# Dense tile pairs of the differential attention spread over the whole mixed attention stream

## What is computed

```
# sparse branch, 8 heads of width 64: compressed keys (32 blocks), all earlier keys, and a window of 512
p_c = masked_softmax(q @ kc.T - slope * dist)          # 32 compressed blocks
p_s = masked_softmax(q @ ks.T - slope * dist)          # all 1024 keys (16 blocks are chosen of 16)
p_w = masked_softmax(q @ kw.T - slope * dist)          # 512 keys back
o_a = g0 * p_c @ vc + g1 * p_s @ vs + g2 * p_w @ vw
# differential branch, 4 heads of width 2 x 64, values of width 128
a   = p[0] - lam * p[1]                                # two causal softmaxes of one head
o_b = rms(a @ vd) * subln * (1 - lam_init)
```

## Time and profile before

| | |
|---|---|
| time before, median of 3 runs | 2198.32 us (2197.31 to 2204.06) |
| the profiled execution: time, span | 2206.14 us, 2204.3 us |
| PE busy over the span | 2027.6 us (92%) |
| DVE, ACT, POOL busy over the span | 1129.4 us (51%), 617.4 us (28%), 114.6 us (5%) |
| mean granted TensorE clock | 0.957 |
| attention stream | from 710 to 1152 us of the span |

### The profile page before, as it was taken

The page is one execution under the profiler, slowest core; times in us unless marked ns, Lnnn a source line. Parts: engine busy times, 40 slices in busy tenths (PEclk is TensorE's granted clock), DMA queues, the critical chain, the costliest instruction groups (busy, mean ns, idle before and its releaser), DMA issues. The chain is left out here.

```text
span 2204.3 us, 33715 instructions
## 1 busy us (share of the span) xinstructions
PE 2027.6 (92%) x12602; PEld 1822.9 (83%) x12602; DVE 1129.4 (51%) x2509; ACT 617.4 (28%) x1220; POOL 114.6 (5%) x176
## 2 busy tenths in 40 slices
PE   6989999998995899999898969699999999999997
PEld 1338888878995788888898957499999999999996
DVE  0434333332235677776766634455555555555555
ACT  2123333421223566775551022211111101111012
POOL 1021000001300000000300000000000000000000
PEclk9989999998996899999999989899999999999998
DMA  9755555321101000000003440311110111101104
GB/s 320 263 187 173 161 150 158 102 80 49 49 1 62 1 1 1 1 1 1 1 15 113 141 144 39 96 58 29 57 57 29 57 38 48 57 29 57 38 1 154
DMA packets 132538, 166.44 MB, mean 76 GB/s; under 512 B 15851, under 2 KB 98635, under 8 KB 132372
## 3 DMA queue, kind: packets, MB, share of 16 engines
q1 hardware_dynamic: 117790, 134.75, 19.2%
q0 software_dynamic: 4832, 17.15, 2.5%
q10 hardware_dynamic: 9808, 13.11, 1.8%
HBM read 144.31 MB, written 22.77 MB: 76 GB/s over the span
## 5 line engine op out<-in xcount | busy, mean ns | idle before, releaser
L1622 DVE TENSOR_TENSOR late_x<-late_x,ffn_po 128x344 f32<-128x344 f32 x528 | 244.3, 509 | 116.0 <-PE ffn_po L1552 115.7
L787 PE MATMUL nsa_out<-zs_z,nsa_probT 128*128 128x64 f32 (+1 forms) x1344 | 179.3, 280 | 5.2 <-DVE zs_z L944 4.9
L1535 PE MATMUL ffn_pg<-late_words_hi,ffn_uhi 128*128 128x344 f32 x528 | 169.3, 321 | 14.6 <-DVE ffn_ulo L1586 14.6
L1496 ACT ACTIVATE ffn_sg<-ffn_pg 128x344 f32<-128x344 f32 x66 | 30.2, 458 | 533.6 <-PE ffn_pg L1535 533.6
L787 PEld LDWEIGHTS nsa_out<-zs_z,nsa_probT 128*128 128x128 f32 x1344 | 172.3, 201 | 8.0 <-DVE zs_z L944 7.8
L1552 PE MATMUL ffn_po<-ffn_a_hi,ffn_ohi 128*128 128x344 f32 x528 | 169.0, 320 | 0.2 <-DVE late_x L1622 0.2
L1535 PE MATMUL ffn_pg<-late_words_lo,ffn_uhi 128*128 128x344 f32 x528 | 169.1, 320 | 0.0
L1535 PE MATMUL ffn_pg<-late_words_hi,ffn_ulo 128*128 128x344 f32 x528 | 169.1, 320 | 0.0
L1552 PE MATMUL ffn_po<-ffn_a_hi,ffn_olo 128*128 128x344 f32 x528 | 168.9, 320 | 0.0
L1535 PE MATMUL ffn_pv<-late_words_hi,ffn_uhi 128*128 128x344 f32 x528 | 168.8, 320 | 0.0
L1535 PE MATMUL ffn_pv<-late_words_lo,ffn_uhi 128*128 128x344 f32 x528 | 168.7, 319 | 0.0
(11 more groups left out here) (452 smaller groups left out, 4520.9 us busy)
## 6 DMA issues: line engine op xcount, KB each, us to landing
mod_wr<-in_w_ada SPq DMA_DIRECT2D x12, 2048.0 KB, 8.9
ffn_raw_u<-in_w_ffn_in SPq DMA_DIRECT2D x44, 512.0 KB, 5.6
kin_kin<-in_cache_kv SPq DMA_DIRECT2D x64, 256.0 KB, 3.5
ffn_raw_o<-in_w_ffn_out SPq DMA_DIRECT2D x22, 512.0 KB, 3.6
gate_d<-dec_gate ACTq DMA_DIRECT2D x48, 172.0 KB, 2.6
late_x<-gate_d SPq DMA_DIRECT2D x8, 1032.0 KB, 5.4
dec_raw<-in_w_in POOLq DMA_DIRECT2D x16, 512.0 KB, 5.5
dec_vin<-in_cache_kv SPq DMA_DIRECT2D x64, 128.0 KB, 2.2
```

Of the source, the lines that this page charges most:

```text
L787: mm = pe.matmul(out[jb.group % 2][:, jb.b, 0:w], probT[t % 2][:, q, :], g.z[:, jb.k0 // P + q, at:at + w], start=(q == 0), stop=(q == til ...
L1496: act.activation(sg[(j + c) % 2][:], pg[(j + c) % 2][:, 0:TCH], ACT.Silu).then_inc(silu_done, 1)
L1535: mm = pe.matmul(bank[b][:, 0:TCH], w[j][:, v * KD + k, :], h[:, k, tok], start=(k == 0 and q == 0), stop=(k == KD - 1 and q == 2))
L1622: dve.tensor_tensor(total[:, k, tok], total[:, k, tok], po[u % 4][:, 0:TCH], ALU.add).then_inc(o_read, 1)
```

## The change

The test for the next dense tile no longer counts all tiles (`group`) but a new counter `done`, which only sparse tiles raise.

```diff
-    p = group = 0
+    p = group = done = 0
...
             group += 1
+            done += 1
             if x == 1:
                 items.append(("two queries", 0))
                 items.append(("two queries", 1))
-            if p < len(pairs) and not due and group * len(pairs) > p * LEAD:
+            if p < len(pairs) and not due and done * len(pairs) > p * LEAD:
                 j, i = pairs[p]
```

## The result

The changed kernel takes 2218.68 us (median of 5 runs, 2216.77 to 2220.23) against 2204.06 us of the kernel before (median of 5 beside it). The ratio is 1.0068 with an interval of 1.0053 to 1.0084: slower by 0.7%, where 0.5% faster was forecast and 2201 us was the upper end of the range. The five include the three of the table ahead of the prediction, whose median of 2198.32 us lies low: in the three later sessions the kernel before had medians of 2205.39, 2205.90 and 2206.01 us. The profiled execution took 2216.77 us with a span of 2215.0 us, 10.7 us longer than that of the kernel before.

A forecast was written before the change was run, and what follows sets the result against it. PE was taken to bound the kernel, with only its idle time and clock to win. Terms 8.8 + 1.7 - 1.5 - 1.0 + 3.0 = 11.0 us gained, from 2198.3 to 2187.3 us; range 2177 to 2201.

The forecast's parts named there:

- What bounds the kernel: Attention stream: PE bounds it, parts with and without dense tiles loaded almost alike; only 42.9 us idle and clock can be won.
- The waits by dense tiles: Five kinds of PE wait in the part with dense tiles, 17.5 us together; half, 8.8 us, forecast gained.
- The crowding: DVE bursts and closely set tiles at head starts; three reasons why spreading dense tiles shortens PE's waits, 8.8 us gained.
- (1): Start of heads 1 to 3: DVE's query remainders, compressed step and a large dense tile no longer stand in one row.
- (2): Sparse and dense tiles in turn: a sparse tile's values get one job more of slack before the finish they wait for.
- (3): Copies after the largest dense tiles: mostly followed by tiles 3, 4 and 5 instead of small tiles 0 and 1.
- the second queries: Second queries' preparation, once directly behind the first queries with no unit between to cover remainders: 1.0 us lost, bounds 0 and 3.6.
- POOL's normalisation: Start of head 6: table scalings find POOL idle, 3.7 us gained; less 2.0 for joins beside POOL, net 1.7 us.
- The cost of joins beside POOL: Joins of D7 and D0 beside POOL's normalisation: 2.0 us lost, bounds 0 and 4.7 us.
- The square root: First root, now straight before the copies of Q6: table load 1.28 and root 0.22 us, whole 1.5 us charged.
- The clock: TensorE at reduced clock in four short stretches of the stream: fewer falls from fewer waits, 3.0 us gained, bounds 8.4 either way.
- B: Rival: slower, 2209 us, by root, normalisation and joins crossing at Q6 in head 5, with two more clock falls; chance 0.10.

The follow-up runs named there:

- LAG 4 kernel: Changed order with every job turned four jobs after its scores instead of three, five probability buffers instead of four; 2192.12 us, ratio 0.9944 to the kernel before.
- the even order: The changed kernel's order of dense and sparse tiles, against the kernel before: 2218.68 us, ratio 1.0068, with every job turned three jobs after its scores.
- LAG 3: Every job turned three jobs after its scores, as in the kernel before (2204.06 us) and the changed kernel (2218.68 us).
- kernel before with join first: Kernel before with the join of a dense tile placed ahead of the maximum of the same job instead of behind it: 2205.95 us, ratio 1.0010.
- LAG 4 in the order before: Kernel before with every job turned four jobs after its scores instead of three, five probability buffers instead of four: 2224.87 us, ratio 1.0096.

## Why the prediction was wrong

**What bounds the kernel: right.** PE bounds the stream, the work of the two parts is alike, and only idle time and clock can change. The account above is this step in numbers: a rest of 361 to 370 us in every kernel of the table.

**The waits by dense tiles: the step that failed.** I set their bounds at 0 and 17.5 us of gain, with "each dense tile brings its waits with it" as the worst. A kind of wait can also grow, and the join's did, by 13.7 us. The sum had 8.8 us gained here, and the sign to watch was that the waits on the copies, the finish, the join and the maxima add up to about 9 us; from 745 us on they were 18.3 and are 28.8. The rows for it were there: the earlier trace rows has the join with the longest wait of these kinds, 1.5 us, and that wait was the one place in the kernel before where the next job but two was not a dense tile (D3 at the end of sparse head 3, s0a behind it):

```profile
997.92 0.31 PE L752 MATMUL nsa_sc<-at_kk,nsa_qhi 128*128 128x128 f32 x1
998.07 0.27 PE L752 MATMUL nsa_sc<-at_kk,nsa_qlo 128*128 128x128 f32 x1
...
999.03 0.75 DVE L986 SCALAR_TENSOR_TENSOR nsa_prob<-nsa_prob,nsa_factor 128x512 f32<-128x512 f32 x1
...
999.84 1.12 PE L769 MATMUL nsa_tp<-g_ident,nsa_prob 128*128 128x128 f32 x4 [1.50 <-DVE nsa_prob L986]
```

I read it as a leftover of crowding. It was the price of a join with little cover, and the change made 26 places with a sparse unit third, 13 of which wait. I had counted how far the finish and the values stand apart, in jobs, and not what PE has to do in the third job.

**The crowding: right, and small.** What reasons (1) and (2) would do is there, though no run takes them apart: finish and maxima fell by 3.9 us. The copies (3) did not fall (6.9 to 7.6 us), and the second queries cost 2.5 us (0.6 to 3.1), where I had 1.0.

**POOL's normalisation: right.** The scalings take 0.28, 0.69 and 0.49 us in all heads now and the 3.7 us are gone, as this view by line shows beside the earlier trace rows:

```profile
L938 DVE TENSOR_TENSOR nsa_share<-nsa_share,a_G x64: 160/161/1680, 749.0 to 1164.1; 128x2 f32<-128x2 f32 x64
...
L1028 DVE TENSOR_SCALAR at_tcmp<-at_tcmp x8: 283/285/288, 717.5 to 1119.7; 128x256 f32<-128x256 f32 x8
L1028 DVE TENSOR_SCALAR at_tsel<-at_tsel x8: 684/688/689, 717.7 to 1119.9; 128x1024 f32<-128x1024 f32 x8
L1028 DVE TENSOR_SCALAR at_twin<-at_twin x8: 486/488/490, 718.3 to 1120.5; 128x640 f32<-128x640 f32 x8
```

The cost of joins beside POOL was almost nil here, by luck: D7 was joined ahead of the normalisation, and D0 in 0.40 us, since the POOL instruction beside it ended 0.25 us after the join began. L938 right behind it took 1.68 us. In the LAG 4 kernel the two did meet, and D0's join took 1.40 us instead of 0.35:

```profile
1035.95 2.37 POOL L734 TENSOR_TENSOR zs_z<-zs_z,c_subln 128x1024 f32<-128x1024 f32 x1
1037.07 1.40 DVE L987 SCALAR_TENSOR_TENSOR nsa_prob<-nsa_prob,nsa_factor 128x128 f32<-128x128 f32 x1
```

The Trainium skill ("GPSIMD Engine Reference", section "8. Key points") says that VectorE instructions with two SBUF inputs contend with GpSimd; the join has two, and this row agrees. It did not decide this change.

**The square root: too dear.** PE waited 1.11 us for the queries at Q6 in head 5, against 1.05 before, and I had put 2.5. The waits for the queries' remainder grew by 2.4 us in all, but mostly in heads 1, 2 and 4.

**The clock: wrong sign.** I expected fewer and shorter waits, so 3.0 us back. The waits became longer (three of at least 1.2 us before, nineteen after, in the list of single waits), and 4.2 us more of the clock went missing: eight falls behind the start-up instead of four. Four of the eight begin within about 2 us of a join wait of 1.4 to 1.7 us (those ending at 901.7, 917.9, 1016.8 and 1035.3 us).

**The rivals.** B was the only one on the right side, but by a crossing at Q6; the run with root and QQ2 moved away was 1.2 us faster, which is within what sessions differ by. The profiled executions differ by 10.7 us of span, with 9.1 of waits and 4.2 of clock less 2.9 of the rest; the medians differ by 14.6, and no trace shows the other 3.9 us.

**The starting time.** I took 2198.3 us, the median of three, while the profiled execution had 2206.1. From the 2204 to 2206 us of later sessions the same sum gives 2193 to 2195, and the measured time stays as far off.

## What to carry to other kernels

When an order of jobs changes under a fixed distance between stages, look at each hand-over and write down what the waiting engine has to do in the jobs between, in microseconds; at a distance of three jobs the third job's scores alone were 2.1 us at one place and 0.4 at another, and all of PE's work after the second job's scores 3.1 or 1.5 us for the same pair of dense tiles. A wait that stands once in the old trace, at the one place that looks like the new order, says the sign of what the new order costs, and only coarsely its size: 1.5 us at 26 places would be 39 us, and 17.3 us in 15 places came of it. Order and distance are to be tried together: the even order lost 0.7% with LAG 3 and won 0.6% with LAG 4, while the old order lost 1.0% with LAG 4.

## What was not expected of the hardware

No single wait of the changed kernel in this stream is longer than 2.1 us, and PE is over 88% busy in it; still TensorE's clock fell to 0.50 again and again, and what this cost (3.4 to 27.3 us over the kernels here) is of the size of what the waits cost. In the changed order with LAG 4 it is 3.4 us, with 30.0 us of waits; in the kernel before with join first it is 12.0 with 29.8. So the sum of the waits does not give the falls. The granted clock of whole executions says the same without the traces: 0.961 to 0.964 in all seven executions of LAG 4 in the changed order, 0.950 to 0.953 in all six of LAG 4 in the order before. Filling the long waits with turns that nobody reads took 10.2 of 17.5 us away, so PE's idleness at these places is a cause; what decides that one cluster of waits brings a fall and its twin in the next head does not stays open.
